# Two sums of weight tiles per MLP round, on VectorE or on GpSimd

## The reference, cut to what matters

```python
for i in range(DEPTH):                    # DEPTH = 2
    ...
    h = rmsnorm(x, g[2])                  # 256 x 2048
    f = jnp.square(jax.nn.relu(h @ mlp_w1[i])) @ mlp_w2[i]    # 2048 x 8192, 8192 x 2048
    x = x + rmsnorm(f, g[3])
```

## Time and profile before

| | |
|---|---|
| median of the runs | 2275.18 us |
| the profiled execution's own time | 2275.38 us |
| its span, from the first to the last instruction | 2273.5 us |
| TensorE busy | 2259.9 us (99%) |
| VectorE busy | 1667.9 us (73%) |
| ScalarE busy | 1328.5 us (58%) |
| GpSimd busy | 105.3 us (5%) |
| mean granted TensorE clock | 0.998 of full speed |

### The profile page before, as it was taken

The page is one execution under the profiler, slowest core; times in us unless marked ns, Lnnn a source line. Parts: engine busy times, 40 slices in busy tenths (PEclk is TensorE's granted clock), DMA queues, the critical chain, the costliest instruction groups (busy, mean ns, idle before and its releaser), DMA issues.

```text
span 2273.5 us, 26585 instructions
## 1 busy us (share of the span) xinstructions
PE 2259.9 (99%) x10609; PEld 1872.6 (82%) x10609; DVE 1667.9 (73%) x2015; ACT 1328.5 (58%) x1769; POOL 105.3 (5%) x138
## 2 busy tenths in 40 slices
PE   9999999999999999999999999999999999999998
PEld 7778788888888888888888888888888888888887
DVE  6675864887788788787878788778788685456664
ACT  6444444666666666665666666666666564444443
POOL 0000000000000000000000000000000010000000
PEclk9999999999999999999999999999999999999999
DMA  9444455799998898996578999989988645644443
GB/s 349 173 165 170 157 186 192 271 286 276 283 317 256 275 295 266 288 276 237 223 281 238 290 288 260 283 282 276 272 279 260 238 147 215 244 178 149 148 161 117
DMA packets 77132, 542.63 MB, mean 239 GB/s; under 512 B 8682, under 2 KB 9013, under 8 KB 13968
## 3 DMA queue, kind: packets, MB, share of 16 engines
q1 hardware_dynamic: 61568, 429.58, 50.2%
q0 software_dynamic: 15296, 111.23, 22.7%
q10 hardware_dynamic: 144, 0.12, 0.0%
HBM read 534.60 MB, written 6.29 MB: 238 GB/s over the span
## 4 chain that ended last, share of the span: by engine, by line
PE 98%; DVE 1%; ACT 0%; issue 0%; ACTq 0%; POOLq 0%; POOL 0%
PE P L353 95%; PE P L356 3%; DVE low L616 0%; DVE X L604 0%; DVE R_h L604 0%; ACT hi L497 0%; ACT R_h L492 0%; DVE st L604 0%; ACT EV L492 0%; ACT EV L523 0%; ACT X L492 0%; DVE R_f_r L601 0%; DVE X L601 0%; ACTq L2656 0%; ACT R_f_r L492 0%
## 5 line engine op out<-in xcount | busy, mean ns | idle before, releaser
L616 DVE TENSOR_TENSOR low<-raw,hi 128x1024 fp32r<-128x1024 f32 (+3 forms) x694 | 813.6, 1199 | 311.0 <-ACT hi L497 306.5
L497 ACT ACTIVATE hi<-raw 128x1024 fp32r<-128x1024 f32 (+3 forms) x694 | 704.7, 1040 | 472.9 <-PE P L353 315.0
L353 PE MATMUL P<-hi,R_h 128*128 128x512 f32 (+2 forms) x2944 | 948.4, 394 | 1.3 <-DVE low L616 0.8
L353 PE MATMUL P<-hi,R_f_r 128*128 128x512 f32 x2480 | 790.9, 391 | 0.1
L353 PEld LDWEIGHTS P<-hi,R_h 128*128 128x128 f32 x2944 | 553.4, 188 | 119.0 <-issue 7.5
L353 PE MATMUL P<-low,R_h 128*128 128x512 f32 (+2 forms) x1472 | 570.9, 388 | 0.0
L353 PEld LDWEIGHTS P<-hi,R_f_r 128*128 128x128 f32 x2480 | 465.6, 188 | 96.4 <-DVE R_f_r L601 0.3
L353 PE MATMUL P<-low,R_f_r 128*128 128x512 f32 x1240 | 482.5, 389 | 0.0
L616 DVE TENSOR_TENSOR low<-R_f,hi 128x1024 fp32r<-128x1024 f32 x226 | 267.4, 1220 | 82.8 <-ACT hi L497 82.3
L353 PEld LDWEIGHTS P<-low,R_h 128*128 128x128 f32 x1472 | 277.2, 188 | 56.2 <-issue 4.3
L353 PEld LDWEIGHTS P<-low,R_f_r 128*128 128x128 f32 x1240 | 233.0, 188 | 47.1
(11 more groups left out here) (220 smaller groups left out, 1391.0 us busy)
## 6 DMA issues: line engine op xcount, KB each, us to landing
raw<-in_w_d SPq DMA_DIRECT2D x128, 1024.0 KB, 7.0
R_f<-in_w_u POOLq DMA_DIRECT2D x84, 1024.0 KB, 10.5
raw<-in_w_u SPq DMA_DIRECT2D x72, 1024.0 KB, 5.4
raw<-in_w_z SPq DMA_DIRECT2D x45, 1024.0 KB, 4.9
raw<-in_w_i SPq DMA_DIRECT2D x36, 1024.0 KB, 4.8
R_f<-in_w_u SPq DMA_DIRECT2D x28, 1024.0 KB, 7.1
X<-in_w_u SPq DMA_DIRECT2D x28, 1024.0 KB, 8.3
raw<-in_w_mo SPq DMA_DIRECT2D x16, 1024.0 KB, 4.8
```

The source lines that it names most:

```text
L353: return self.e.matmul(o, l, r, start=start, stop=stop, skip_group_check=True)
L497: self.e.activation(hi, raw, ACT.Copy).then_inc(*self.inc("high_made", ("high", k, d)))
L616: self.e.tensor_tensor(low, raw, hi.bitcast(f32), ALU.subtract).then_inc(*self.inc("low_made", *lows))
```

## The change

`tile_sum` moves from VectorE's class to GpSimd's, at the same place in the order of the program: there it is a `tensor_tensor` on `self.e`, now GpSimd, and tells of its end by the semaphore `pow_done`, not `dve_done`. The buffer of the ring was freed by the end of the sum, behind which VectorE's `low` of the same tile had always been made. Now it is freed when both have ended.

```diff
--- before.py
+++ after.py
@@ class Dve
-    def tile_sum(self, o, i, ready, done):
-        self.wait_ge(ready)
-        self.tt(o, o, i, ALU.add, done)
-
@@ class Pool
     def times_row_apart(self, dst, src, row, ready, done):
         self.wait_ge(ready)
         self.e.tensor_tensor(dst, src, row, ALU.mult).then_inc(*self.inc("pow_done", done))
+
+    def tile_sum(self, o, i, ready, done):
+        self.wait_ge(ready)
+        self.e.tensor_tensor(o, o, i, ALU.add).then_inc(*self.inc("pow_done", done))
@@ def third_sum(j):
                 if not listing:
-                    freed[landed] = done
+                    freed[landed] = [done, ("low", k, 3)]
                     load_ahead()
```

## The result

The changed kernel takes 2294.63 us (median of 4 runs, 2293.51 to 2297.62) against 2275.14 us before, a ratio of 1.0089 (95% interval 1.0077 to 1.0101): 19.5 us slower by the medians. The profiled execution took 2293.51 us, its span is 2291.7 us, 18.2 us more than before. The forecast was 2275.4 us with no change as the likeliest case; the range ended at 2291 us. All ratios here are of the fast runs and can differ from the quotient of the medians in the fourth digit; one execution of the changed kernel, when it was run once more, took 2869.75 us at a mean granted clock of 0.75 and is left out.

What follows compares the result with a forecast made beforehand. TensorE, busy 99% of the span and never idle in the long windows of rounds, was taken as the bound. Relief of VectorE, GpSimd's sums, loads and waits each counted 0, giving 2275.4 us, range 2274.0 to 2291 us.

Steps and rivals of the forecast that it cites:

- The length of a sum: One 128 x 2048 sum on GpSimd was taken as 4.4 us, within 3.5 to 5.2.
- The start in GpSimd's queue: GpSimd's sums can start at 639.4, behind the accumulating DMA issued at 638.55, nine microseconds before VectorE did them; cost 0.
- The distances: How long before TensorE uses them the lows are ready: 5.5 us for down 2's second half, 6.9 for up 3's first.
- rival 1: Engines exclude each other and alternate; up 3 waits 0.25 to 0.55 us a round, from 4.13 us a sum; chance 0.30.
- three changes of hand: Some 0.1 us each time the turn passes between GpSimd and VectorE, raising up 3's wait from 0.25 to 0.55 us.
- The ring's earlier loads: The ring's buffers are freed sooner, so SyncE may load 4 to 5 us earlier; costed at 0.
- the wait on two names: A buffer is freed by the later of sum and low; SyncE's queue is held until 648.4 at most; cost 0.
- no exclusion: Neither engine holds the other while GpSimd adds beside VectorE's five lows; cost 0, part of a joint chance of 0.57.
- sharing that the distance covers: Both engines share and each stretches by less than the 5.5 us of distance; cost 0, part of a joint 0.57.
- rival 3: Engines exclude each other, VectorE keeps the turn while it has lows; down 3 in time, 0 us, within the joint 0.57.
- The row beside L984: Beside GpSimd's L984, VectorE ran seven operations with one PSUM input, 0.27 us each, none with two SBUF tensors.
- Rival 2: GpSimd keeps the turn through both sums; down 2's second half is 1.74 us late, 14 rounds 24 us, 2300 us; chance 0.07.

## Why GpSimd kept the turn in three rounds

**A wait between the sums:**

```diff
-                E.tile_sum(..., [("linked", l, e, j), ("loaded", k)], done)
+                E.tile_sum(..., [("linked", l, e, j), ("loaded", k)] + ([("chained", l, e, 4, 0)] if j else []), done)
```

> The changed kernel with one wait more: the second sum of a round waits for the first one's end. Theory (where GpSimd kept the turn through both sums, its second instruction had begun on some of its cores before the first had ended on all, so VectorE found no gap): with the wait no low is held for more than about 5.7 us, the rounds with 2 to 8 us of loss are gone or down to 3 us, in all 2279 to 2286 us. Rival (VectorE's place in the turn is decided by something else): still lows of 8 us and more in some rounds, 2290 us or more.

Measured: 2284.12 us (ratio 1.0042, 1.0027 to 1.0057). In the first round the low that was held for 8.32 us is held for 3.80, and the second sum waits for it:

```profile
473.30 4.94 POOL L984 TENSOR_TENSOR X<-X,raw 128x2048 f32<-128x2048 f32 x1
478.41 5.39 POOL L984 TENSOR_TENSOR X<-X,raw 128x2048 f32<-128x2048 f32 x1 [0.17 <-POOL X L984]
...
475.54 3.80 DVE L616 TENSOR_TENSOR low<-raw,hi 128x1024 fp32r<-128x1024 f32 x1 [1.97 <-ACT hi L497]
479.26 5.63 DVE L616 TENSOR_TENSOR low<-raw,hi 128x1024 fp32r<-128x1024 f32 x1
```

Up 3 is 0.9 us late in the first and the eighth round and 2.8 us in the seventh; the steady rounds stay at 0.37 us (the ninth loses 0.6). One low of the seventh is held for 6.32 us, more than the 5.7 that were expected: it is the one that was overtaken, held for the first sum from its start. The two mechanisms come apart: without GpSimd's double turns the change costs 9.8 us, with them 19.5.

**Both sums in two parts** (8 columns, a wait on them, the other 2040; the second sum's small part waits for nothing of the first sum; no wait between the sums):

```diff
+        self.e.tensor_tensor(o[:, 0:8], o[:, 0:8], i[:, 0:8], ALU.add)
+        self.wait_ge(self.own)
+        self.e.tensor_tensor(o[:, 8:2048], o[:, 8:2048], i[:, 8:2048], ALU.add)
```

> The changed kernel with each sum in two instructions, the first 8 columns, and then, after a wait on these, the other 2040. The second sum's small part does not wait for the first sum. Theory (GpSimd's cores come out of step because some of them still write the descriptors of the DMA issued 0.6 us before the first sum, and only thus does the second sum begin before the first has ended): the wait brings them in step, and no round has GpSimd keep the turn through both: no low over 6.4 us, 2280 to 2287 us. Rival (they are out of step anyhow, or the second sum can always slip in): lows of 8 us and more in some rounds, 2290 us or more.

Measured: 2282.57 us (ratio 1.0031, 1.0019 to 1.0042), 28 held lows, none over 5.6 us. But this splits the second sum as well, so it does not tell whether the wait ahead of the first or the split of the second did it.

**Only the first sum in two parts:**

```diff
+        if small:                                   # the first sum of a round
+            self.e.tensor_tensor(o[:, 0:8], o[:, 0:8], i[:, 0:8], ALU.add)
+            self.wait_ge(self.own)
+            o, i = o[:, 8:2048], i[:, 8:2048]
         self.e.tensor_tensor(o, o, i, ALU.add)
```

> The changed kernel with the first sum of a round in two instructions, 8 columns and then, after a wait on these, 2040; the second sum is one instruction and waits for nothing of the first. Theory (GpSimd's cores are in step after the wait, so that the second sum cannot begin on some of them before the first has ended on all): no round in which it keeps the turn through both sums, no low over 6.4 us, 2280 to 2287 us. Rival (what brought VectorE its turn in the runs before was the wait between the sums or the split of the second): rounds 1 and 8 have a low of 8 us again and lose 2.6 us or more, 2286 us or more.

Measured: 2284.85 us (ratio 1.0043, 1.0026 to 1.0060); 28 held lows, the longest 5633 ns. The first round again, GpSimd and the two lows:

```profile
473.51 4.61 POOL L988 TENSOR_TENSOR X<-X,raw 128x2040 f32<-128x2040 f32 x1
478.08 5.59 POOL L988 TENSOR_TENSOR X<-X,raw 128x2048 f32<-128x2048 f32 x1
...
475.13 4.08 DVE L616 TENSOR_TENSOR low<-raw,hi 128x1024 fp32r<-128x1024 f32 x1 [1.94 <-ACT hi L497]
479.13 5.63 DVE L616 TENSOR_TENSOR low<-raw,hi 128x1024 fp32r<-128x1024 f32 x1
```

The first sum's large part found the way free here too (the low before it ended at 473.19), and nothing stands between it and the second sum, and still VectorE got its turn. What differs from the changed kernel is that GpSimd had come to a stop before the first sum, and did not begin it 0.6 us after issuing a DMA. In the seventh round, the low that was overtaken in the changed kernel is not held at all. That fits the reading that the second sum can begin on a part of GpSimd before another part has ended the first when the DMA's issue has put these out of step. The overlap of the two sums' rows fits it too: it was 0.21 us in the first round of the changed kernel (472.66 + 4.93 against 477.38), and is 0.04 us here (473.51 + 4.61 against 478.08) and 0.06 us at most in any round of this run. The Trainium skill, GPSIMD Engine Reference, section 2.1, says that each of the engine's cores starts the next instruction as soon as its own share is done, and section 4 that a pair of them writes the descriptors of a DMA. No row shows the cores one by one, so the reading is supported by three runs and these overlaps and not shown. What puts GpSimd out of step is argued only: this run changed both the stop and the distance to the DMA's issue, and none changed the DMA alone.

**The change once more:**

> The changed kernel once more, for a second profile. Theory: the eleven or so steady rounds are 83.8 us long again; rounds 1 and 8 again have GpSimd keep the turn through both sums and lose 2.6 us or more; the loss of 7.8 us of round 7 depends on which engine comes first by tenths of a us, so it stands in other rounds or in none: 2288 to 2298 us. Rival (round 7 is slow by what it does): the same 7.8 us in round 7.

Measured: 2296.44 us (ratio 1.0092, 1.0075 to 1.0109). Its profile has the same three costly rounds, with 4.2, 7.8 and 4.2 us, and in these the two sums' rows overlap by 0.23, 0.39 and 0.22 us, in the others by 0.03 or 0.04. The part of the expectation on the seventh round missed: it is the seventh again. In this profile and in the changed kernel's, ScalarE makes the hi ahead of down 2's first low 0.3 us later in that round than in the others (idle for 0.77 us before it, not 0.48), and so that low comes 0.26 us before the sum and not 0.55 or more. In the run with one sum on each engine this delay stood in the twelfth round. What delays ScalarE by 0.3 us there is open. The first round, by contrast, lost 2.6 us in one profile and 4.2 in the other with the same idle time of 2.3 us. The windows after it, of the changed kernel and of this run, show the difference:

```profile
483.00:487.00 4.00, 3.72 (x16) 3.11 (x17) 4.00 (x5) 0.00 (x0) 0.00 (x0) 1.00 0.64 219
```

```profile
484.00:487.00 3.00, 2.35 (x6) 1.89 (x7) 3.00 (x4) 0.00 (x0) 0.00 (x0) 0.62 0.42 106
```

The granted clock stayed at 1.00 once and fell to a mean of 0.62 the other time, towards its lower level of 1.2 GHz. An idle time of 2.3 us cost 2.6 us at the full clock, and 4.2 us where the clock fell.

## Why the prediction was wrong, by its steps

- The bound (TensorE is never idle in a round, nothing to win): right, shown by the run without the sums.
- The length of a sum, 4.4 us with 3.5 to 5.2: right. In a steady round the second takes 4.48 us from the end of the low before it to its own end, and 4.62 us when it stands alone (in the run with the second sum late). The 4497 ns of the Trainium skill (GPSIMD Engine Reference, section 3.1), which the prediction quotes, agree with these to 3%.
- The start in GpSimd's queue, right behind the DMA issue: right. In the steady rounds it starts 0.6 to 0.8 us before up 5.
- The distances, 5.5 and 6.9 us, and the point from which rival 1 decides: right. Up 3 was 0.27 us late where 0.55 was priced for rival 1. The 0.1 us for each of three changes of hand were a guess, and no run shows them: a held low ends 1.08 or 1.09 us after GpSimd's sum, where I had put 1.23 and a change of hand. The ring's earlier loads and the wait on two names cost nothing that the rounds show.
- The step that failed is the choice between exclusion and none, made in the part on what the two engines do to each other. The forecast of 0 us rested on no exclusion, or on sharing that the distance covers, or on rival 3, and I gave these 0.57 together. What the runs showed: the engines exclude each other by whole instructions, lows of 1.22 us are held for 4.0 to 10.8 us, and TensorE waits. Rival 3 never occurred: VectorE got one low between the sums, or none. The row beside L984 could not speak for or against exclusion: it has operations with an input in PSUM, and these pass in the changed kernel too. But that the trace never shows the two together was wrong. The 14 small sums of L989 on GpSimd are in the earlier trace rows with 0.54 to 0.94 us, and I took only their smallest. Four of them are of 128 x 1. Timelines of the kernel before, VectorE and GpSimd, for two of these:

```profile
398.88 0.68 DVE L616 TENSOR_TENSOR low<-raw,hi 128x512 fp32r<-128x512 f32 x1
399.06 0.94 POOL L989 TENSOR_TENSOR st<-st,half 128x1 f32<-128x1 f32 x1 [117.25 <-DVE st L609]
...
404.15 0.54 POOL L989 TENSOR_TENSOR st<-st,half 128x1 f32<-128x1 f32 x1 [4.15 <-DVE st L609]
404.24 0.35 DVE L604 SCALAR_TENSOR_TENSOR R_h<-P,cols,R_h 128x128 fp32r<-128x128 f32 x1 [0.17 <-ACT R_h L492]
```

  Beside operations with an input in PSUM they last 0.54 and 0.56 us, beside lows 0.94 and 0.82 us, and both of the latter end 0.43 us after the low that ran when they were issued. Two rows are little, but they pointed at exclusion, and the length of GpSimd's smallest sum depends on what VectorE does.
- The one statement that the prediction had on exclusion was the rule of the Trainium skill, SBUF — State Buffer, "Who interferes with whom", and I gave the two rivals that follow from it 0.30 and 0.07. The rule holds in this kernel: a held low waits for a whole instruction of GpSimd that reads SBUF, and not for one that only writes. "In turn", as I put it, held in eleven rounds; in three, GpSimd had two turns running.
- The second failure is a term's size. Rivals 1 and 2 were priced as if one of them ruled all 14 rounds. Both occurred, 1 in eleven rounds for 4.1 us and 2 in three for 14.5 us. Rival 2 was priced at 1.74 us a round from up 3's and down 2's tiles alone. It cost 2.6 to 7.8. The 2.6, in the first round at the full clock, are the same path with other lengths: the first sum could begin 0.4 us later there, when down 2's first low had ended (472.93, up 5 at 472.64), and the two sums took 9.2 us and not 8.8. Above that, two things were not in the price: that the held low can be the one before, with the R_m<-P,R_m behind it in VectorE's queue for which down 2 also waits, and that TensorE's granted clock falls to half after an idle time of 2.3 us (in three of four cases, over the two profiles) or within one of 4.9 us (in both). The range's upper end left all of it out.

## What to carry to other kernels

Before moving an elementwise operation from VectorE to an idle GpSimd, list what VectorE does in that time with both inputs in SBUF, and hold the length of GpSimd's instruction, twice if two stand in a row, against the time by which these are early. Look in the trace for small instructions of GpSimd too, and at what VectorE did beside those that last longer than their like. An engine that is 20% idle can lose more by being held 5 us at a bad place than it wins by being relieved of 4.6 us. Where TensorE is fed without a gap, price an idle time of 2 us and more with the slower clock behind it.

## What the runs showed of the hardware that I had not expected

- Reading one tensor on GpSimd holds VectorE's two-input instruction like reading two: 2.79 us of copy, 2.83 us of low. Writing alone does not: 1.82 us memsets beside lows of 1.22.
- Two GpSimd instructions in a row can hold VectorE through both, 8.3 and 10.8 us, though it had been waiting since the first or was issued 0.26 us before it. A wait of GpSimd on its own small instruction ahead of the first, or between the two, ended that: 5.6 us at most with the first, 6.3 us with the second.
- The same idle time of TensorE, 2.3 us, was followed by the full clock in one execution and by a mean of 0.62 over the next 3 us in another.
- A GpSimd sum of 128 x 1 lasts 0.54 or 0.56 us beside VectorE operations with an input in PSUM, and 0.82 or 0.94 us beside two-input ones from SBUF.
- Where GpSimd kept VectorE out through two sums, their rows overlap by 0.21 to 0.39 us, in six of six cases; where it did not, by 0.06 us at most.
